# Latents stage written out and skewed by one tile, with attention's row maxima spread over the units

## The reference, cut to what matters

```python
def mla_queries(u, q_norm_g, w_uq, qk_g_q):
    q = (rmsnorm(u, q_norm_g) @ w_uq).reshape(B, L, 8, 64 + 32)
    return rmsnorm(q[..., :64], qk_g_q[:64]), rmsnorm(q[..., 64:], qk_g_q[64:])
def mla_keys(u, kv_norm_g, w_ukv, qk_g_k):
    c_kv, k_rope = u[..., :256], u[..., 256:]
    kv = (rmsnorm(c_kv, kv_norm_g) @ w_ukv).reshape(B, L, 8, 64 + 64)
    k_nope, v = kv[..., :64], kv[..., 64:]
    return rmsnorm(k_nope, qk_g_k[:64]), rmsnorm(k_rope, qk_g_k[64:]), v
def attend(q_nope, q_rope, k_nope, k_rope, v):
    s = einsum('bqhn,bkhn->bhqk', q_nope, k_nope) + einsum('bqhr,bkr->bhqk', q_rope, k_rope)
    return einsum('bhqk,bkhv->bqhv', softmax(s * MLA_SCALE), v)
```

## Time and profile before

| | us |
|---|---|
| median of 3 runs (3706.1 to 3716.2) | 3712.27 |
| the profiled execution | 3705.01 |
| its span in the profile | 3703.4 |
| latents stage (537.9 to 727.4) | 189.5 |
| attention (727.4 to 1087.6) | 360.2 |
| TensorE busy, whole span | 3292.6 |

### The profile page before, as it was taken

The page is one execution under the profiler, slowest core; times in us unless marked ns, Lnnn a source line. Parts: engine busy times, 40 slices in busy tenths (PEclk is TensorE's granted clock), DMA queues, the critical chain, the costliest instruction groups (busy, mean ns, idle before and its releaser), DMA issues. The chain is left out here.

```text
span 3703.4 us, 38116 instructions
## 1 busy us (share of the span) xinstructions
PE 3292.6 (89%) x15050; PEld 2528.5 (68%) x15050; DVE 1614.9 (44%) x1944; ACT 945.9 (26%) x1079; POOL 321.7 (9%) x231
## 2 busy tenths in 40 slices
PE   5879987589965588999999999989996999999999
PEld 1338864344535467888888888867775778888887
DVE  5214305646638864222333332357666333333233
ACT  2223112133331022211111111157765231111111
POOL 2000000046640011000000000020000100000000
PEclk8879998779987798999999999989998999999999
DMA  6761210000021131111111111111112211111112
GB/s 251 281 244 64 89 52 0 0 0 1 1 99 76 44 133 34 35 40 35 35 37 38 36 40 35 40 68 34 42 37 80 74 40 46 45 51 45 51 45 74
DMA packets 46018, 228.88 MB, mean 62 GB/s; under 512 B 6776, under 2 KB 7288, under 8 KB 39641
## 3 DMA queue, kind: packets, MB, share of 16 engines
q1 hardware_dynamic: 42456, 205.86, 15.8%
q10 hardware_dynamic: 1728, 13.63, 0.9%
q0 software_dynamic: 1728, 7.87, 0.5%
HBM read 201.65 MB, written 25.69 MB: 61 GB/s over the span
## 5 line engine op out<-in xcount | busy, mean ns | idle before, releaser
L240 PE MATMUL bank<-h_hi,w_hi 128*128 128x512 f32 (+1 forms) x2616 | 705.0, 370 | 13.1 <-DVE h_lo L1563 8.2
L240 PE MATMUL bank<-h_lo,w_hi 128*128 128x512 f32 (+1 forms) x2616 | 704.0, 369 | 8.3 <-issue 8.3
L240 PE MATMUL bank<-h_hi,w_lo 128*128 128x512 f32 (+1 forms) x2616 | 702.7, 369 | 0.0
L226 DVE TENSOR_TENSOR w_lo<-w_raw,w_hi 128x1024 fp32r<-128x1024 f32 x194 | 262.7, 1354 | 674.9 <-ACT w_hi L220 670.5
L240 PEld LDWEIGHTS bank<-h_hi,w_hi 128*128 128x128 f32 x2616 | 453.8, 189 | 100.6 <-issue 15.7
L240 PEld LDWEIGHTS bank<-h_lo,w_hi 128*128 128x128 f32 x2616 | 454.1, 189 | 95.2 <-issue 9.6
L240 PEld LDWEIGHTS bank<-h_hi,w_lo 128*128 128x128 f32 x2616 | 454.1, 189 | 85.8
L1495 DVE SCALAR_TENSOR_TENSOR x<-bank,c_mods,x 128x1024 f32<-128x1024 f32 (+3 forms) x280 | 271.8, 1006 | 256.7 <-PE bank L240 256.6
L220 ACT ACTIVATE w_hi<-w_raw 128x1024 fp32r<-128x1024 f32 x194 | 203.9, 1052 | 648.0 <-PE bank L240 608.8
L240 PE MATMUL bank<-hid_hi,w_hi 128*128 128x512 f32 (+1 forms) x880 | 242.7, 373 | 11.6 <-DVE x L1495 11.6
L240 PE MATMUL bank<-hid_lo,w_hi 128*128 128x512 f32 (+1 forms) x880 | 240.7, 371 | 0.0
(11 more groups left out here) (280 smaller groups left out, 3722.6 us busy)
## 6 DMA issues: line engine op xcount, KB each, us to landing
w_raw<-in_weights SPq DMA_DIRECT2D x194, 512.0 KB, 3.5
ada_w<-in_ada_w SPq DMA_DIRECT2D x32, 1536.0 KB, 7.7
x<-in_x SPq DMA_DIRECT2D x2, 5120.0 KB, 18.7
h_gate<-u_scratch SPq DMA_DIRECT2D x4, 2560.0 KB, 10.1
u_scratch<-uc POOLq DMA_DIRECT2D x12, 640.0 KB, 3.2
spec_lat<-f_spec ACTq DMA_DIRECT2D x2, 3584.0 KB, 10.4
h_spec<-spec_lat SPq DMA_DIRECT2D x2, 3584.0 KB, 17.1
x_kept<-x SPq DMA_DIRECT2D x1, 4096.0 KB, 13.6
```

Of the source, the lines that this page charges most:

```text
L226: e.tensor_tensor(k.w_lo[s][:, :], k.w[s][:, :], k.w_hi[s][:, :].bitcast(F32), ALU.subtract).then_inc(k.split_lo[s], 1)
L240: mm = e.matmul(out[:, c:c + m], w[:, c1:c1 + P], x[:, c:c + m], start=(first and kk == 0 and n == 0), stop=(last and kk == kt - 1 and n = ...
```

## The change

In *latents* the loop is written out. TensorE's order becomes products(0), then for each further tile products(t), turn(t - 1), and turn(9) at the end, with the waits for free banks split in one for the query banks and one for the key banks. POOL's copies go: products and squares read `lat` and `rope` in place. ScalarE's copy of the turned queries of tile t - 1 stands inside its steps of tile t, behind the squares; VectorE's copy of the turned keys of tile t - 1 stands between the variance steps and the reciprocal of tile t. Weights, gains and cosines are loaded by POOL in *even_in*, once the last normalised input tile is made, and the gains are folded at the end of VectorE's queue there; only the sines are loaded in *latents*. The buffers of keys, queries and values move to other places in SBUF.

In *attention* the score blocks of the next head stand at units 0, 2, 4, ... 14, 16, 17, and the spreads and row sums later; VectorE's maxima come one at a time with one other step between two of them; the normalisation is cut in halves and runs one head later; the score blocks 0 to 7 of head 0 alternate between two sets of banks; and ScalarE writes the constant edge rows. At the end the context's queries of the last head are scaled ahead of the others.

```diff
 # even_in, vector: behind the last split
+            fold_gains(k, e)
 # even_in, gpsimd: ahead of its loop of stores
+            e.wait_ge(k.xr_ready, norm.h_base + KT)
+            latent_inputs(k, e)
...
+def latent_inputs(k, e):
+    d = k.d
+    for t, name in ((k.wq, "w_uq"), (k.wkv, "w_ukv")):
+        e.dma_start(t[:, :, :], d[name]).then_inc(k.m_landed, 16)
+    e.dma_start(k.gq[:, :], d["gq"]).then_inc(k.m_landed, 16)
+    e.dma_start(k.gk[:, :], d["gk"]).then_inc(k.m_landed, 16)
+    e.dma_start(k.cos[:, :, :], d["cos"]).then_inc(k.m_landed, 16)
+def fold_gains(k, e):
+    e.wait_ge(k.m_landed, 80)
+    for kk in range(3):
+        e.tensor_scalar(k.wq[:, kk, :], k.wq[:, kk, :], k.g_lat[:, kk:kk + 1], None, ALU.mult).then_inc(k.m_folded, 1)
+    for kk in range(2):
+        e.tensor_scalar(k.wkv[:, kk, :], k.wkv[:, kk, :], k.g_lat[:, 3 + kk:4 + kk], None, ALU.mult).then_inc(k.m_folded, 1)
 # latents, tensor
+            def products(t):
+                s, cols = t % 2, slice(t * P, (t + 1) * P)
+                if t >= 2:
+                    e.wait_ge(q_out, t - 1)
...
+                if t >= 2:
+                    e.wait_ge(k_out, t - 1)
...
+            e.wait_ge(k.m_folded, 5)
+            products(0)
+            for t in range(1, NT):
+                products(t)
+                turn(t - 1)
+            turn(NT - 1)
 # latents, scalar
+                e.activation(sqr[:, :], k.bank[:, 4 * s + 1, 384:384 + ROPE], ACT.Square).then_inc(hsq, 1)
+                if t:
+                    queries_out(t - 1)
+                e.activation(v[:, t, :].rearrange("p (b h c) -> p b h c", b=2, c=VD), kvps(s)[:, :, :, NOPE:],
+                             ACT.Copy, scale=st[:, 5:6]).then_inc(vout, 1)
 # latents, vector
+                e.tensor_scalar(ss[:, 16:25], ss[:, 16:25], 1.0 / ROPE, EPS, ALU.mult, ALU.add).then_inc(hss, 1)
+                if t:
+                    keys_out(t - 1)
+                e.wait_ge(hsd, t + 1)
 # attention
-    MAX_AT = [1, 2, 7, 8, 9, 11, 12, 13, 16, 17]
-    SPREAD_AT = [4, 10, 14, 16, 19]
-    SUMS_AT, REFILL_AT = 4, 16
+    MAX_AT = [0, 2, 4, 6, 8, 10, 12, 14, 16, 17]
+    SPREAD_AT = [7, 11, 15, 17, 19]
+    SUMS_AT, REFILL_AT = 5, 16
+    score_sums = lambda h, j: k.acc[j % 2 if h == 0 and j < 8 else 0]
 # attention, tensor, spread
-                e.wait_ge(mx_done, h * NT + 2 * p + 2)
+                e.wait_ge(mx_done, h * NT + 2 * p + 2 if h or p == 4 else 8)
 # attention, vector
+            for h in range(1, HEADS):
+                maximum(h, 0)
+                low_k(h)
+                maximum(h, 1)
+                low_q(h)
+                maximum(h, 2)
+                if h >= 2:
+                    invert(h - 2, 0)
+                maximum(h, 3)
+                if h >= 2:
+                    invert(h - 2, 1)
+                maximum(h, 4)
+                if h >= 2:
+                    scale(h - 2, 0)
+                    scale(h - 2, 1)
+                maximum(h, 5)
+                if h >= 2:
+                    invert_ctx(h - 2)
+                maximum(h, 6)
+                if h >= 2:
+                    scale_ctx(h - 2)
+                for j in range(7, NT):
+                    maximum(h, j)
 # attention, scalar, at the start (the memsets of vector go)
+            for n in range(2):
+                e.activation(row96(k_hi[n]), ones, ACT.Copy).then_inc(edges, 1)
+                e.activation(row96(k_lo[n]), ones, ACT.Copy, scale=0.0).then_inc(edges, 1)
+                e.activation(row96(q_lo[n]), ones, ACT.Copy, scale=0.0).then_inc(edges, 1)
```

More of the change, by code:

```diff
@@ L843, in latents @@
     ss = k.at("hs", at + 4456, [P, 32])
[L844 to L849, removed]
+    t1 = k.at("rot1", S0 + 1280, [P, HEADS, ROPE])
+    t2 = k.at("rot2", S0 + 1536, [P, HEADS, ROPE])
+    sin_landed, sq_ready = k.sem("m_sin"), k.sem("m_sq")
+    sums, trq_full, trk_full = k.sem("m_sums"), k.sem("m_trq"), k.sem("m_trk")
     ms, sd, hsq, hss, hsd, vout, tok = (k.sem("m_" + n) for n in ("ms", "sd", "hsq", "hss", "hsd", "v", "tok"))
-    freed = [k.sem(f"m_freed{s}") for s in range(2)]
+    q_out, k_out = k.sem("m_q_out"), k.sem("m_k_out")
     steps_sem = k.sem("m_steps")
@@ L860, in _ @@
         def _(e):
[L861 to L874, removed]
+            e.dma_start(sin[:, :, :], d["sin"]).then_inc(sin_landed, 16)
@@ L876, in _ @@
+            e.wait_ge(sin_landed, 16)
         @block.tensor
         def _(e):
[L878 to L900, removed]
-                        e.transpose(k.bank[0:QD, 4 * s + h // 4, (h % 4) * P:(h % 4 + 1) * P], qb[:, s, h, :], k.ident[:, :])
-                    for h in range(HEADS):
-                        mm = e.transpose(k.bank[0:QD, 4 * s + 2 + h // 4, (h % 4) * P:(h % 4 + 1) * P], kb[:, s, h, :],
-                                         k.ident[:, :])
-                    mm.then_inc(tr_full, 1)
@@ new lines, in turn @@
+            def turn(t):
+                s = t % 2
+                e.wait_ge(tok, t + 1)
+                e.wait_ge(vout, t + 1)
+                for h in range(HEADS):
+                    mm = e.transpose(k.bank[0:QD, 4 * s + h // 4, (h % 4) * P:(h % 4 + 1) * P], qb[:, s, h, :], k.ident[:, :])
+                mm.then_inc(trq_full, 1)
+                for h in range(HEADS):
+                    mm = e.transpose(k.bank[0:QD, 4 * s + 2 + h // 4, (h % 4) * P:(h % 4 + 1) * P], kb[:, s, h, :],
+                                     k.ident[:, :])
+                mm.then_inc(trk_full, 1)
@@ L1180, in _, with maximum, low_k @@
         def _(e):
-            def low(h):
+            def maximum(h, j):
+                e.wait_ge(s_full, h * NT + j + 1)
+                e.reduce_max(mx[:, h % 2, j:j + 1], score_sums(h, j)[:, 0:T if j < 8 else CTX], AX_X).then_inc(mx_done, 1)
+            def low_k(h):
                 e.wait_ge(hi_ready, 2 * h + 1)
@@ L1187, in low, with invert @@
                                 ).then_inc(lo_ready, 1)
-            def maxima(h, first, end):
-                for j in range(first, end):
-                    e.wait_ge(s_full, h * NT + j + 1)
-                    e.reduce_max(mx[:, h % 2, j:j + 1], k.acc[0][:, 0:T if j < 8 else CTX], AX_X).then_inc(mx_done, 1)
-            def normalise(h):
-                own = slice(64 * (h % 2), 64 * (h % 2) + 64)
+            def invert(h, c):
                 e.wait_ge(slot_read, sum_slot[h] + 1)
-                e.reciprocal(rs[:, :], rs[:, :]).then_inc(ri_ready, 1)
-                e.wait_ge(ri_ready, 2 * h + 1)
+                part = rs[:, c * CTX:(c + 1) * CTX]
+                e.reciprocal(part, part).then_inc(ri_ready, 1)
@@ new lines, in scale_ctx @@
+            def scale_ctx(h):
+                e.wait_ge(ci_ready, h + 1)
+                e.tensor_tensor(attT[64 * (h % 2):64 * (h % 2) + 64, h // 2, LAT:T], ctx_raw[0:64, :], ctx_ri[0:64, :],
+                                ALU.mult).then_inc(ctx_done, 1)
+            maximum(0, 0)
+            maximum(0, 1)
+            low_k(0)
+            maximum(0, 2)
+            maximum(0, 3)
+            low_q(0)
+            for j in range(4, NT):
+                maximum(0, j)
+            for h in range(1, HEADS):
[21 more added lines that the diff above has]
+                    maximum(h, j)
```

264 lines of the change are left out of this document (130 added, 134 removed).

## The result

The kernel after took 3593.41 us, median of 4 runs (3587.24 to 3597.48), beside 3709.18 us for the kernel before in as many runs (3701.7 to 3716.2): a ratio of 0.9687, 95% interval 0.9662 to 0.9712. The profiled execution took 3592.84 us, its span 3591.2.

What follows compares the result with a forecast made beforehand. TensorE, busy 89% of the span, was taken as the bound, its standstills as the gain. Savings of 52.2 + 14.7 + 27.4 + 1.3 + 1.2 = 96.8 us, off the 3712.3 us median, gave 3615.5 us; own range 3602 to 3628.

Steps and rivals of the forecast that it cites:

- The other 3154 us of the span I take as unchanged.: Whole kernel: everything outside the terms for latents and attention keeps its time, 3154 us.
- Rival 4: Whole kernel: straight-line code starves an engine of instructions and eats the gain, no measurable change; chance 0.01.
- the six heads: Attention: heads without waits for maxima take 36.4 us each at full clock, 218.4 for six; 27.4 us saved.
- the floor of 36.05 us a head: Attention's six heads: the best case for a head's time, the bound at which 29.5 us are saved.
- The latents: Latents stage: two-tile alternation gives way to 12.4 us a tile; 137.3 us against 189.5, 52.2 saved.
- The half clock behind the first turn: Latents: 1.7 us added for products at half clock after TensorE's short standstills.
- So TensorE sets the pace: Latents, steady state: TensorE's turn and products take 12.4 us a tile, VectorE's chain close under it at 11.6.
- The opening: Attention's start: maxima run back to back, first unit starts at 747.4, not 762.07; 14.7 us saved.
- The low parts: Attention's heads: VectorE's low parts of keys and queries take 2.56 us each, so no score waits.
- Rival 1: Attention's heads: low parts take 3.75 us, maxima still wait, clock falls; only 5.5 us saved there, 3637 us; chance 0.12.
- rival 2: Latents: engines still take turns, chain and turn add to 15.0 us a tile; 3639 us; chance 0.07.
- Rival 3: Latents: half clock through the stage, 124 us more, kernel slower at 3739 us; chance 0.02.

Runs made afterwards that it cites:

- The six places: Kernel before with 0 or 240 added TensorE instructions: first ffn 979.2, 968.4 us; kernel after with 0, 16, 128, 256: 965.9, 979.7, 962.7, 965.8 us.
- old_units: Kernel after with score blocks, spreads and row sums at their old units, VectorE's order still new: attention 345.9 us, beside 308.7.
- late_load: Kernel after with weights, gains and cosines loaded, and gains folded, at the start of the latents again: latents 149.8 us, beside 137.4.
- q_halves: Kernel after with ScalarE's copy of the turned queries in two halves, each with its own release: latents 131.6 us, whole time 3588.14 us, ratio 0.9677.
- grouped_dve: Kernel after with VectorE's steps of a head grouped as before, units at the new places: attention 398.2 us, beside 308.7.

## Why the prediction was wrong, point by point

**The step that failed** is "The other 3154 us of the span I take as unchanged." The first ffn took 13.3 us less, nearly all of it by the place of its loop; with those 13.3 us back the time would be 3606.7 us, inside the range. By the spans the forecast was 15.4 us short (112.2 less 96.8; by the medians 19.0): 13.3 of the ffn, 6.9 of attention, and 4.9 the other way in prologue and hyena. The forecast time itself, 3615.5 us, was 22.1 too high, 3.1 of them because the kernel before took 3709.2 us here and not 3712.3. Rival 4 had the mechanism, straight-line code and the fetching of instructions, with the wrong place and the wrong sign: it looked at the code that became straight, where no stall for issue came up, and not at a loop that was moved by it. The six places show that the place is the cause; a chance of 0.01 for anything to do with instruction fetch was too low.

**The term that was mis-sized** is the six heads: 35.2 us for 27.4. The mechanism was right, scores without waits and a clock of 1.00, but the floor of 36.05 us a head was the busy time of a head with three waits in it (35.99). Without waits the same 156 products were busy for 34.85 us. Part of what a wait costs was in my floor as busy time: six times 0.9 us. The 0.4 for leftovers was not needed either. old_units confirms the price from the other side, 2.0 us for each us waited. One reason given for the change was wrong and cost nothing: the normalisation does not run a head later than before, both kernels invert the row sums of head h - 2 among the maxima of head h (first 14.4 us into the second head before, at 16.0 after).

**The latents** came out at 137.4 us for 137.3, and partly by chance. The start (12.4 us by late_load, for 13.0), the two waits for VectorE and the last turn at half clock (3.6 us) were as forecast, and the round was 12.32 for 12.4. The half clock behind the first turn, 1.7 us in the sum, cost 2.3 in this profile and nothing in some others, so the same latents took 135.0 to 137.4 us. But I took the turn at 3.44 us from the earlier trace rows, where the clock was at its lower level; at 2.4 GHz it is 1.9. The query copy ends 3.3 us behind the sums, as I had it (3.4), and the turn at 1.75: so TensorE waits the difference, 1.58 us. An error of 1.5 us and a wait of 1.6 cancelled. The claim "So TensorE sets the pace" is wrong: the way over ScalarE does, as q_halves shows by 0.42 us a round.

**The opening** gave 14.4 us for 14.7 (and lost 0.7 in its first units), the first head 1.3 for 1.3, the end 1.3 for 1.2.

**The low parts**, my uncertain price, were 2.59 and 2.41 us for 2.56. Rival 1 needed 3.75 and did not come. Of rival 2 the condition came true, the query copy was late by 1.58 us a tile, but not the consequence: it added only itself, and products and turns ran beside VectorE's chain. Rival 3 did not come either; the clock was 0.94.


## What to carry to other kernels

Unrolling one stage moves every loop behind it in the instruction stream of its engine, and here one of the loops changed its time by it: look in the stages that were not touched for waits without a releaser behind a loop's return, and if they are there move the loop by added instructions in a place where they are hidden (128 and 240 led to good places here, 16 to a bad one). A busy time read from a stretch with waits in it is no floor, and a duration read at the lower clock is no duration for the higher one: take both from a stretch in which the engine was never idle. Where two engines' rounds are within a microsecond, follow each release through every engine, since the one that holds the pace may be a third that is idle most of the time.

## What the runs showed of the hardware that was not expected

TensorE's stall behind a taken branch depends on where the loop lies: at most 0.7 us at four of the six places, 1.7 to 2.3 us at two, with the clock at 0.88 over the 14 us about it; together 3.0 us a return (697.0 us for 685.0 over four returns).

A semaphore increment in TensorE's queue took about 0.15 us when many stood in a row (240 of them from 1093.3 to 1130.2, 256 from 992.0 to 1031.3).

A VectorE instruction with two SBUF inputs that meets POOL's work can wait for more than one of its instructions. Before, a low part started at 885.99, POOL ran a cast until 887.16 and went on with an add; the low part took 3.76 us, for 1.49 alone. The 64x256 multiplication of grouped_dve waited through two casts and an add. The Trainium skill ("SBUF — State Buffer", "Who interferes with whom") has the later of the two engines wait until the earlier one's instruction ends; by that the multiplication would have cost at most 0.42 + 1.25 us (an estimate, own time and the cast it met), and the measured 3.70 goes beyond it.
